# Moving the memory projections behind the second input unit, and the router's closing arithmetic into the first pair of experts

## The reference, cut to what matters

```python
mk = (mem_prompt @ w_mem_k[l]).reshape(b, n_mem, MEM_HEADS, HEAD_DIM)
mv = (mem_prompt @ w_mem_v[l]).reshape(b, n_mem, MEM_HEADS, HEAD_DIM)
q, k, v, h, g_b, g_c, qm, gate_a, gate_c, gate_m = _split_in(x @ w_in)
...
logits = jnp.dot(xt, w_router) + b_router
top_v, top_i = lax.top_k(logits, TOP_K)
top_w = jax.nn.softmax(top_v, axis=-1)
gates = jnp.sum(jax.nn.one_hot(top_i, N_EXPERTS) * top_w[..., None], axis=1)
for e in range(N_EXPERTS):
    y = y + gates[:, e:e + 1] * _swiglu(xt, wg[e], wu[e], wd[e])
```

## Time and profile before

| | |
|---|---|
| median of 3 runs | 1580.06 us |
| the profiled execution | 1580.78 us |
| its span, first to last instruction | 1579.0 us |
| granted TensorE clock, mean | 0.993 |
| PE busy | 1532.7 us (97%) |
| PEld busy | 1353.5 us (86%) |
| DVE busy | 1118.7 us (71%) |
| ACT busy | 922.3 us (58%) |
| DMA | 416.61 MB, mean 264 GB/s |

### The profile page before, as it was taken

How to read it: one execution, slowest core, us unless ns; L and a number is a source line. 1 busy time by engine, 2 the same in 40 slices (tenths; PEclk the granted TensorE clock), 3 DMA queues, 4 the chain that set the end, 5 groups by cost and what they waited for, 6 DMA issues and landing times.

```text
span 1579.0 us, 22606 instructions
## 1 busy us (share of the span) xinstructions
PE 1532.7 (97%) x8937; PEld 1353.5 (86%) x8937; DVE 1118.7 (71%) x1023; ACT 922.3 (58%) x958; POOL 151.2 (10%) x190
## 2 busy tenths in 40 slices
PE   7999999999999899999899999999999999999996
PEld 7989899899999799999678888888888888888785
DVE  5546647644444635666688888888888888888987
ACT  4545444433333654444577777777777777767775
POOL 4103003300002103000530000000000000030000
PEclk9999999999999999999999999999999999999998
DMA  9747344874445345433689999999999999999981
GB/s 309 256 125 228 110 132 138 340 240 138 153 141 159 92 141 175 135 107 107 235 296 393 390 384 357 375 381 389 378 349 381 383 388 371 351 390 373 391 316 60
DMA packets 226424, 416.61 MB, mean 264 GB/s; under 512 B 8592, under 2 KB 110368, under 8 KB 224752
## 3 DMA queue, kind: packets, MB, share of 16 engines
q1 hardware_dynamic: 217712, 383.28, 69.1%
q0 software_dynamic: 8608, 31.89, 5.7%
HBM read 393.99 MB, written 23.11 MB: 264 GB/s over the span
## 4 chain that ended last, share of the span: by engine, by line
PE 90%; DVE 4%; DMA 2%; ACT 2%; issue 1%; POOL 1%; SPq 0%; POOLq 0%; ACTq 0%; DVEq 0%
PE ps L1761 12%; PE ps L1762 12%; PE ps L1763 12%; PE ps L2215 10%; PE ps L2217 10%; PE ps L2216 10%; PE ps L2199 5%; PE ps L2201 5%; PE ps L2200 5%; PE ps L2226 1%; DMA mem_v<-in_cache_mem_v_dram 1%; DMA raw<-in_w_mem_k_dram 1%; PE ps L1958 1%; PE ps L1799 1%; PE ps L1829 1%
## 5 line engine op out<-in xcount | busy, mean ns | idle before, releaser
L1230 DVE TENSOR_TENSOR low<-raw,high 128x2048 fp32r<-128x2048 f32 x264 | 603.7, 2291 | 91.1 <-ACT high L900 89.7
L900 ACT ACTIVATE high<-raw 128x2048 fp32r<-128x2048 f32 x264 | 505.9, 1919 | 201.1 <-PE ps L2217 128.0
L1240 DVE TENSOR_TENSOR low<-raw,high 128x2048 fp32r<-128x2048 f32 (+1 forms) x91 | 206.1, 2267 | 204.9 <-ACT high L893 204.8
L1761 PE MATMUL ps<-xh,high 128*128 128x320 f32 x1088 | 342.8, 315 | 7.4 <-DVE xl L1437 6.9
L1762 PE MATMUL ps<-xh,low 128*128 128x320 f32 x1088 | 337.7, 310 | 0.0
L1763 PE MATMUL ps<-xl,high 128*128 128x320 f32 x1088 | 337.5, 310 | 0.0
L2215 PE MATMUL ps<-high,xeh 128*128 128x512 f32 (+1 forms) x768 | 292.4, 381 | 2.8 <-DVE low L1230 1.8
L2217 PE MATMUL ps<-high,xel 128*128 128x512 f32 (+1 forms) x768 | 289.4, 377 | 0.0
L2216 PE MATMUL ps<-low,xeh 128*128 128x512 f32 (+1 forms) x768 | 288.1, 375 | 0.0
L893 ACT ACTIVATE high<-raw 128x2048 fp32r<-128x2048 f32 (+1 forms) x91 | 172.3, 1893 | 161.3 <-PE ps L1763 139.9
L1761 PEld LDWEIGHTS ps<-xh,high 128*128 128x128 f32 x1088 | 206.0, 189 | 16.5 <-issue 14.1
(11 more groups left out here) (362 smaller groups left out, 1620.4 us busy)
## 6 DMA issues: line engine op xcount, KB each, us to landing
raw<-in_exp_w_gate_dram SPq DMA_DIRECT2D x88, 1024.0 KB, 7.4
raw<-in_exp_w_up_dram SPq DMA_DIRECT2D x88, 1024.0 KB, 7.4
raw<-in_exp_w_down_dram SPq DMA_DIRECT2D x88, 1024.0 KB, 6.7
raw<-in_w_in_dram SPq DMA_DIRECT2D x37, 1024.0 KB, 5.3
ybuf<-zeros POOLq DMA_DIRECT2D x12, 1024.0 KB, 17.7
raw<-in_ffn_w_gate_dram SPq DMA_DIRECT2D x11, 1024.0 KB, 5.3
raw<-in_ffn_w_up_dram SPq DMA_DIRECT2D x11, 1024.0 KB, 5.3
raw<-in_w_o_dram SPq DMA_DIRECT2D x8, 1024.0 KB, 5.1
```

The source lines that it names most:

```text
L900: act.activation(high[(N_DENSE + m) % HI_RING][:, :], raw_moe[s][:, :], ACT.Copy).then_inc(hi_done, 1)
L1230: dve.tensor_tensor(low_moe[s][:, :], raw_moe[s][:, :], high[(N_DENSE + m) % HI_RING][:, :].bitcast(F32), ALU.subtract).then_inc(lo_done, 1)
L1240: dve.tensor_tensor(low[n % RING][:, cols], raw[n % RING][:, cols], high[n % HI_RING][:, cols].bitcast(F32), ALU.subtract).then_inc(lo_don ...
L1761: pe.matmul(out, wh, ah, start=first, stop=False)
```

## The change

Two edits. First, `STREAM` puts the memory units behind `z` unit 1 instead of unit 0; the memory transposes stay after unit 0, `memory()`, which loses them on all three engines, is called after unit 1, and slots 0 and 1 of layer 0 are both worked off behind it (`work_beside`). Second, in the router, five DVE instructions that count the rounds and eight that make the gates go into `rounds_and_gates()`, called at step 6 of the first pair, and `places()` is called at step 11; ACT's wait and exponential go from before the `residual` copies to behind the last `gathered`.

```diff
-STREAM = layer_units(0)[:1] + MEM_UNITS + layer_units(0)[1:] + ffn_units() + layer_units(1)
+STREAM = layer_units(0)[:2] + MEM_UNITS + layer_units(0)[2:] + ffn_units() + layer_units(1)
...
+GATES_AT, PLACES_AT = 6, 11
...
+def work_beside(l, i):
+
+    if l == 0 and i <= 1:
+        return SLOTS[0] + SLOTS[1] if i == 1 else []
+    return SLOTS.get(i, ())
...
@@ ACT, mixer @@
                     if l == 0 and i == 0:
+                        for k in range(X_STARTS, len(START)):
+                            start_part(k)
+                        continue
+                    if l == 0 and i == 1:
                         memory()
-                    for work in SLOTS.get(i, ()):
+                    for work in work_beside(l, i):
@@ ACT, router @@
-            act.wait_ge(rt_diff, 1)
-            act.activation(pair[:, :, 1:2], pair[:, :, 0:1], ACT.Exp).then_inc(rt_exp, 1)
...
             for c in range(1, 4):
                 gathered(0, c, FIRST_BANK[c], 1.0)
+            act.wait_ge(rt_diff, 1)
+            act.activation(pair[:, :, 1:2], pair[:, :, 0:1], ACT.Exp).then_inc(rt_exp, 1)
             act.activation(row_f[:, 2:3], eps[:, 0:1], ACT.Copy).then_inc(e_silu, 1)
@@ DVE, mixer @@
                     if l == 0 and i == 0:
+                        for k in range(X_STARTS, len(START)):
+                            start_part(k)
+                    lo(UNIT_OF[u] + AHEAD)
+                    if l == 0 and i == 0:
+                        continue
+                    if l == 0 and i == 1:
                         memory()
-                    else:
-                        lo(UNIT_OF[u] + AHEAD)
@@ DVE, router @@
             link(dve.tensor_reduce(cnt[:, 0:1], ps[:, 1, 56:64], AX, ALU.max))
-            link(dve.tensor_scalar(cnt[:, 1:2], cnt[:, 0:1], 128.0, float(PAIRS), ALU.is_gt, ALU.mult))
...
-            dve.tensor_copy(total_i[:, :], cnt[:, 3:4]).then_inc(rt_total, 1)
             for c in range(4):
                 tokens_lo(0, c, FIRST_BANK[c], 1.0)
...
-            dve.wait_ge(rt_exp, 1)
-            link(dve.tensor_scalar(pair[:, :, 2:3], pair[:, :, 1:2], 1.0, None, ALU.add))
...
-            places()
+            def rounds_and_gates():
+
+                link(dve.tensor_scalar(cnt[:, 1:2], cnt[:, 0:1], 128.0, float(PAIRS), ALU.is_gt, ALU.mult))
+                link(dve.tensor_scalar(cnt[:, 2:3], cnt[:, 0:1], 256.0, float(PAIRS), ALU.is_gt, ALU.mult))
+                link(dve.tensor_tensor(cnt[:, 3:4], cnt[:, 1:2], cnt[:, 2:3], ALU.add))
+                link(dve.tensor_scalar(cnt[:, 3:4], cnt[:, 3:4], float(PAIRS - 3), None, ALU.add))
+                dve.tensor_copy(total_i[:, :], cnt[:, 3:4]).then_inc(rt_total, 1)
+                dve.wait_ge(rt_exp, 1)
+                link(dve.tensor_scalar(pair[:, :, 2:3], pair[:, :, 1:2], 1.0, None, ALU.add))
+                link(dve.reciprocal(pair[:, :, 2:3], pair[:, :, 2:3]))
+                link(dve.tensor_tensor(pair[:, :, 3:4], pair[:, :, 1:2], pair[:, :, 2:3], ALU.mult))
+                dve.tensor_tensor(oh1[:, :, :], oh1[:, :, :], wide(pair[:, :, 2:3]), ALU.mult)
+                link(dve.tensor_tensor(oh2[:, :, :], oh2[:, :, :], wide(pair[:, :, 3:4]), ALU.mult))
+                for k in range(ROUNDS):
+                    last = dve.tensor_tensor(gates[:, :, NE * k:NE * k + NE], oh1[:, :, :], oh2[:, :, :], ALU.add)
+                link(last)
@@ DVE, pair_of_experts @@
+                    if first and m == GATES_AT:
+                        rounds_and_gates()
+                    if first and m == PLACES_AT:
+                        places()
@@ PE, mixer @@
-                    if n == 0:
+                    if l == 0 and i == 0:
+                        pe.wait_ge(ld_mem, 2 * 16)
+                        for k in range(X_STARTS, len(START)):
+                            start_part(k)
+                        continue
+                    if l == 0 and i == 1:
                         memory()
-                    for work in SLOTS.get(i, ()):
+                    for work in work_beside(l, i):
```

More of the change, by code:

```diff
@@ L918, in memory @@
             def memory():
-                for k in range(X_STARTS, len(START)):
-                    start_part(k)
                 for n, u in enumerate(MEM_UNITS):
@@ L1278, in memory @@
             def memory():
-                for k in range(X_STARTS, len(START)):
-                    start_part(k)
-                lo(AHEAD)
                 for n, u in enumerate(MEM_UNITS):
@@ L1616, in _ @@
             link(dve.tensor_reduce(cnt[:, 0:1], ps[:, 1, 56:64], AX, ALU.max))
-            link(dve.tensor_scalar(cnt[:, 1:2], cnt[:, 0:1], 128.0, float(PAIRS), ALU.is_gt, ALU.mult))
-            link(dve.tensor_scalar(cnt[:, 2:3], cnt[:, 0:1], 256.0, float(PAIRS), ALU.is_gt, ALU.mult))
-            link(dve.tensor_tensor(cnt[:, 3:4], cnt[:, 1:2], cnt[:, 2:3], ALU.add))
-            link(dve.tensor_scalar(cnt[:, 3:4], cnt[:, 3:4], float(PAIRS - 3), None, ALU.add))
-            dve.tensor_copy(total_i[:, :], cnt[:, 3:4]).then_inc(rt_total, 1)
             for c in range(4):
@@ L1785, in memory @@
             def memory():
-                pe.wait_ge(ld_mem, 2 * 16)
-                for k in range(X_STARTS, len(START)):
-                    start_part(k)
                 pe.wait_ge(start_lo, len(START))
```

## The result

The changed kernel takes 1586.27 us (median of 6 runs, 1585.52 to 1587.82) against 1579.88 for the kernel before (6 runs): a ratio of 1.0042, 95% interval 1.0032 to 1.0051. It is slower by 6.4 us. The forecast of 1584.3 (1579 to 1588) has the side right; its time is 2 us short, and its change, 2.1 + 1.45 = 3.55 us, lacks 2.8. The profiled execution took 1585.59 us. One of six later runs of the changed kernel, with the granted clock at 0.751 instead of 0.99, took 1890.81 us and is left out of what follows.

A forecast was written before the change was run, and what follows sets the result against it. PE, busy 97% of the span, was taken as the bound. The profiled 1580.78 us plus 2.1 for edit one and 1.45 for edit two (-3.5 + 1.7 + 2.4 + 0.85) gave 1584.3, range 1579 to 1588.

The forecast's parts named there:

- gain in front: Ahead of the first memory unit: PE's 3.14 us idle and the 1.7 lost to the clock behind it go, 4.8 won.
- new wait: PE at job 0's probabilities' transposes (L1858): waits about 5.5 us, resumes at 68.3 against 67.65; clock drop adds 1.7.
- landing of the memory values: Exponentials on ACT wait for it, starting 6.2 us behind the last memory copy; up to 1.4 more allowed for slower landing.
- third unit's wait: Third expert unit: PE's 1.84 us wait for `lo` and the 1.7 clock loss behind it go, gain 3.5.
- joined stretch: Ahead of the first expert unit: idle 1.41 and 0.98 become one 2.4 us, nothing gained in length, clock loss +1.7.
- blocks: DVE, first expert pair: 2.2 us at step 6 and 3.6 at step 11, 1.7 free each; cost 0.5 + 1.9 = 2.4.
- half a fall, 0.85: Behind the 1.9 us wait at step 11 of the first pair: clock loss counted at half, +0.85 us.
- rival 4: First pair's second half: POOL's scatters crowd the full weight stream, PE waits up to 7 us: 1591; 6%.
- mask arithmetic: In `memory()` on DVE: it and the first key copy come later, but PE wants that copy later still; costed at nothing.
- Rival 2: First pair: DVE's moved 2.2 and 3.6 us find cover, PE never waits for them: 1581.0; 12%.
- Rival 3: Faster: rivals 1 and 2 both hold and the memory values land 1 us sooner: 1576.7; 10%.
- Rival 1: Clock stays at 2.4 GHz behind the router's 2.4 and 1.9 us stretches: 1581.8, or 1580.1 if at L1858 too; 18%.

The follow-up runs named there:

- keys' landing only: Changed kernel, with the first exponentials waiting for the stores of the memory keys alone, not the values: 1583.66 us, ratio 1.0020 to the kernel before.
- repaired edit two: Kernel before plus the router edit, its moved DVE work in five pieces and the exponential in its old place: 1577.76 us, ratio 0.9983.
- probabilities ahead of `lo`: Changed kernel, with DVE normalising job 0 behind unit z2 ahead of the low part of unit 8: 1581.49 us, ratio 1.0003 to the kernel before.
- early exponential: Changed kernel, with ACT's exponential back ahead of the `residual` copies: 1583.02 us, ratio 1.0015 to the kernel before.

## Why the prediction was right, and where it was short

**Edit one: +2.1 forecast, +4.2 measured.** The gain in front came as foretold. Of the new wait every step but one was right. ACT's timeline of after:

```profile
60.75 0.48 ACT L983 ACTIVATE sc<-ps,small 128x256 f32<-128x256 f32 x1 [11.43 <-DMA out_mem_v_prompt_dram<-mv]
...
62.56 1.03 ACT L941 ACTIVATE mem_kT<-ps 128x1024 f32<-128x1024 f32 x1
63.46 1.93 ACT L903 ACTIVATE high<-raw 128x2048 fp32r<-128x2048 f32 x1
...
71.19 1.02 ACT L963 ACTIVATE pT<-ps 128x1024 f32<-128x1024 f32 x1 [3.77 <-PE ps L1872]
```

And DVE's:

```profile
52.67 0.69 DVE L1296 COPY mv<-ps 128x512 f32<-128x512 f32 x1 [1.03 <-PE ps L1815]
...
65.42 2.29 DVE L1252 TENSOR_TENSOR low<-raw,high 128x2048 fp32r<-128x2048 f32 x1 [7.73 <-ACT high L903]
...
67.84 1.23 DVE L1347 TENSOR_TENSOR sc<-sc,small 128x1024 f32<-128x1024 f32 x1
```

From the last memory copy to PE's arrival the forecast had 62.8 - 53.7 = 9.1; it is 69.21 - 7.45 - 52.67 = 9.09. From the exponentials to the probabilities' transposes it had 68.3 - 59.9 = 8.4; it is 69.21 - 60.75 = 8.46: copy, `hi`, `lo` and `normalise` one behind the other. **The step that failed is the landing of the memory values**, "they started 57.84 - 51.63 = 6.2 us behind the copy": it is 60.75 - 52.67 = 8.08, past the upper bound of 1.4 more. The DMA view of ten us around the copy (busy tenths of the queues in 40 slices), and the landings of the last two stores (us from issue), before, from 51 to 61:

```profile
DMA  0000001968989999999999998000000995030000
...
DMA to landing us min/median/max: 4.5/4.6/4.6
```

and after, from 52 to 62, with the one packet of instructions (packets, MB, share) that the view has from 58 to 60.7:

```profile
DMA  9999866976798989999999999110100099500000
...
DMA to landing us min/median/max: 4.7/5.6/6.5
...
q8 instruction: 1, 0.02, 2.2%
```

Full queues alone do not explain the 1.9: from the issue of the stores on (52.61 in before, 53.65 in after) the queues are busy in both. The two stores report with 32 semaphore marks. Thirty of them are in at 59.42, 5.24 behind the last issue (before: 4.37), the last two only at 60.35 and 60.67, 6.49 behind it (4.61). They belong to four packets of 4 KB that start at 59.17, when a packet of 16 KB which the trace calls instruction, not data, is through (58.23 to 59.19). In all nine profiled executions with edit one such a packet lies there, and the last mark comes 1.07 to 1.80 us behind the thirtieth; in the three with the old front the packet comes after the landing, and the last mark is 0.15 to 0.24 behind the thirtieth. So 0.9 of the 1.9 is a delay of all pieces (0.2 to 0.7 in the other eight), and 1.0 the wait of the last ones behind that packet. This is read from the order in the twelve traces; no run moved the packet alone, and why it comes sooner with edit one stays open. That the landing is in the chain is shown (58.20 with the keys' landing only). The fall was foretold at 1.7 and is 1.9. Sum: 2.1 + 1.9 + 0.2 = 4.2.

**Edit two: +1.45 forecast, +2.4 measured.** Every place was right. The third unit's wait went with its fall, -3.5. The exponential won nothing, as `e_silu` stands behind the same sum; ACT's timeline of after:

```profile
794.24 1.28 ACT L1171 ACT_TABLE_LOAD   x1
...
795.65 0.19 ACT L1172 ACTIVATE row_f<-eps 128x1 f32<-128x1 f32 x1
```

PE starts 0.44 behind that row, before 0.45 (793.65 against 793.20), and the joined stretch, forecast at 2.4, is 2.50 with its fall. The blocks, on DVE's timeline:

```profile
819.45 0.14 DVE L1657 TENSOR_SCALAR cnt<-cnt 128x1 f32<-128x1 f32 x1
...
821.60 2.29 DVE L1242 TENSOR_TENSOR low<-raw,high 128x2048 fp32r<-128x2048 f32 x1
...
834.45 0.16 DVE L1639 COPY top<-topf 128x3 f32<-128x3 f32 x1
...
838.06 4.48 DVE L1242 TENSOR_TENSOR low<-raw,high 128x2048 fp32r<-128x2048 f32 x2
```

They take 2.15 and 3.61 (2.2 and 3.6 forecast) and make PE wait 0.56 and 1.80 (0.5 and 1.9 forecast): of each block 1.6 and 1.8 us were free, against the 1.7 of the forecast. **The step that failed is "half a fall, 0.85"** behind the 1.9: in both profiled executions of after it came whole, and the granted clock of the others, 0.989 to 0.991, gives no sign of less. -3.5 + 1.7 + 2.4 + 1.7 = 2.3.

With the two misses, 1.9 and 0.85, the sum of 1584.3 becomes 1587.1. That the measured 1586.3 is 0.8 nearer is luck: the sum starts from the profiled execution, 1580.78, which stands 0.9 above the median of before, 1579.88. That the time lies in the range is luck in part too: the landing passed its own bound, and the bounds of the blocks were not needed.

**What was costed at nothing.** The scatters now occupy POOL from 838.5 to 852.9 instead of 799.4 to 813.8 (833 to 847 forecast), their transfers landed in 7.9 us at the median, and no PE wait follows the 840.40; rival 4 is out, and the repaired edit two confirms it. The first of them:

```profile
838.53 2.77 POOL L871 DMA_INDIRECT ybuf<-acc,topi  x1 [45.57 <-issue]
```

The mask arithmetic on DVE ahead of the first key copy kept its cover: no idle stretch stands between 28.81 and the 7.45.

**The rivals.** Rival 2, the blocks hidden, is out: 0.56 and 1.80. Rival 3 needed an earlier landing and got a later one. Rival 1, the clock staying up, is out for the changed kernel, where the clock fell behind all three stretches in both profiled executions; in other kernels it stayed up behind one or the other. The Trainium skill (TensorE: Matmul & The Clock Gate, "HAM oscillation — how this bites in real kernels"), by which only longer stretches take the clock down, is contradicted by the 2.50 and the 1.80 here, and the measurement decides. What the prediction foretold of the trace came so but for two: the wait at the probabilities is 7.45 and not 5 to 6, and `z` unit 3 comes not within 1 us of its old time but 3.1 later (73.89 against 70.79).

## What to carry to other kernels

A unit of matrix work that moves away takes its cover with it: before moving it, walk the next consumer's chain on every engine in program order, and price a landing in it by its last piece, with room for it to come later than in the nearest row (here 1.9 us). Here that chain (landing, copy, `hi`, `lo`, `normalise`) could be cut in two places, by the order of one call and by a semaphore for the keys alone, which turned 4.2 us lost into 1.8 to 3.4 won (67.63 and 66.10 against 69.45). Small work on an engine that runs a two-step pipeline is free in pieces shorter than its slack (up to 1.6 us here) and costs its excess, and the clock's fall, in one block.

## What the runs showed that I had not expected

Whether an idle stretch of PE costs the clock is not settled by its length alone. Over the twelve profiled executions (behind the first 12 us, and up to the last product): stretches up to 1.42 us were never followed by a fall; those of 1.78 to 1.84 in 8 of 11 cases; those of 2.50 in 6 of 7; those of 2.67 and more always. One of 1.62 lay inside a fall. The same 1.84 at the same unit cost a fall in before and none with edit one alone. Each fall lasts 3.41 us or twice that. So a forecast for one stretch of about 2 us is good to 1.7 us per execution, and a median over several runs holds a mixture: of the twelve runs with the probabilities ahead of `lo`, the two with a mean granted clock of 0.995 took 1577.54 and 1578.87 us, the three with 0.991 took 1582.37 to 1583.66. Nor is the mixture the same for every kernel, as the early exponential shows. The Trainium skill (TensorE: Matmul & The Clock Gate, "Part 1: The HAM clock gate") has the gate run freely against the kernel. The runs agree with it, in that executions of one kernel differ in their clock, as those twelve do.
